# Value products of head pairs of 64: both heads in the column halves, in plain single precision

## What is computed

```python
# a: chunked attention over 9 chunks of 64 keys, with a relative bias (4 heads)
sc = einsum(qc, kb) * d ** -0.5 + bias
o = einsum('bhcqk,bckhd->bcqhd', softmax(sc), vb)
# b: each query attends the keys that an indexer picked (4 heads)
att = einsum('bqhd,bqkhd->bhqk', qb, ks) * scale
o = einsum('bhqk,bqkhd->bqhd', softmax(att), vs)
# d: neighbourhood of 8 rows by 16 columns plus 256 context keys (8 heads, odd layer)
p = softmax(concatenate([s_loc + bias, s_ctx]))
o = einsum(p_loc, vs) + einsum(p_ctx, vc)
```

## Time and profile before

| | |
|---|---|
| median of 3 runs | 4104.63 us (4094.35 to 4112.15) |
| profiled execution | 4107.38 us, span 4105.6 us |
| mean granted TensorE clock | 0.934 of 2.4 GHz |
| TensorE busy | 3635.7 us, 89% |
| weight loads | 3008.8 us, 73% |
| VectorE busy | 2167.0 us, 53% |
| ScalarE busy | 1415.1 us, 34% |
| POOL busy | 237.5 us, 6% |
| DMA | 230.08 MB, mean 56 GB/s |

### The profile page before, as it was taken

The page is one execution under the profiler, slowest core; times in us unless marked ns, Lnnn a source line. Parts: engine busy times, 40 slices in busy tenths (PEclk is TensorE's granted clock), DMA queues, the critical chain, the costliest instruction groups (busy, mean ns, idle before and its releaser), DMA issues. The chain is left out here.

```text
span 4105.6 us, 46423 instructions
## 1 busy us (share of the span) xinstructions
PE 3635.7 (89%) x19222; PEld 3008.8 (73%) x19222; DVE 2167.0 (53%) x3943; ACT 1415.1 (34%) x2519; POOL 237.5 (6%) x343
## 2 busy tenths in 40 slices
PE   7999998886989999999898888888698888988788
PEld 5888876765768888888676676776686777776667
DVE  4599944555734322323555655655535556525563
ACT  3211254444222211112345434444424445423441
POOL 1021110000100000000000000000000000000000
PEclk9699999898999999999899998988798999989999
DMA  3223330001521111111210011000221000110112
GB/s 111 96 93 127 120 118 23 28 21 60 181 83 48 51 36 52 52 46 40 90 34 23 23 33 32 27 28 22 80 74 65 31 30 30 37 31 8 32 34 95
DMA packets 69571, 230.08 MB, mean 56 GB/s; under 512 B 8744, under 2 KB 12840, under 8 KB 69360
## 3 DMA queue, kind: packets, MB, share of 16 engines
q1 hardware_dynamic: 43056, 132.68, 9.8%
q0 software_dynamic: 22848, 81.85, 5.8%
q10 hardware_dynamic: 3456, 12.58, 0.8%
HBM read 180.42 MB, written 36.17 MB: 53 GB/s over the span
## 5 line engine op out<-in xcount | busy, mean ns | idle before, releaser
L2388 PE MATMUL PS<-m,m 128*128 128x512 f32 (+3 forms) x3560 | 1413.2, 398 | 125.7 <-ACT m L2597 22.2
L2389 PE MATMUL PS<-m,m 128*128 128x512 f32 (+3 forms) x3560 | 1375.6, 388 | 0.0
L2390 PE MATMUL PS<-m,m 128*128 128x512 f32 (+3 forms) x3560 | 1373.4, 387 | 0.0
L2388 PEld LDWEIGHTS PS<-m,m 128*128 128x128 f32 (+2 forms) x3560 | 684.8, 193 | 304.0 <-ACT m L2597 31.3
L2390 PEld LDWEIGHTS PS<-m,m 128*128 128x128 f32 (+2 forms) x3560 | 686.0, 193 | 135.6 <-issue 1.6
L2389 PEld LDWEIGHTS PS<-m,m 128*128 128x128 f32 (+2 forms) x3560 | 688.8, 194 | 117.3 <-issue 2.3
L2735 DVE TENSOR_TENSOR m<-m,m 128x1024 fp32r<-128x1024 f32 (+5 forms) x204 | 210.2, 1031 | 400.2 <-ACT m L2573 399.5
L3021 DVE TENSOR_TENSOR m<-PS,m 128x512 fp32r<-128x512 f32 x352 | 240.9, 689 | 296.6 <-ACT m L2665 296.2
L2665 ACT CAST m<-PS 128x512 fp32r<-128x512 f32 x352 | 205.4, 589 | 495.9 <-PE PS L2495 494.4
L2486 PE MATMUL PS<-m,m 64*128 64x256 f32 (+5 forms) x1968 | 253.7, 369 | 70.6 <-ACT m L2654 54.1
L2486 PEld LDWEIGHTS PS<-m,m 64*128 64x128 f32 (+1 forms) x1968 | 214.8, 199 | 115.3 <-ACT m L2654 69.2
(11 more groups left out here) (196 smaller groups left out, 3897.0 us busy)
## 6 DMA issues: line engine op xcount, KB each, us to landing
m<-in_w SPq DMA_DIRECT2D x220, 512.0 KB, 3.5
g_scratch<-m ACTq DMA_DIRECT2D x24, 512.0 KB, 2.6
m<-g_scratch POOLq DMA_DIRECT2D x24, 512.0 KB, 4.7
m<-in_w SPq DMA_DIRECT2D x32, 256.0 KB, 2.6
x_scratch<-m POOLq DMA_DIRECT2D x2, 4096.0 KB, 13.5
m<-m POOLq DMA_DIRECT2D x60, 128.0 KB, 2.7
m<-in_xT POOLq DMA_DIRECT2D x24, 256.0 KB, 7.0
y_scratch<-m POOLq DMA_DIRECT2D x12, 512.0 KB, 2.9
```

Source lines behind the costliest of these rows:

```text
L2388: pe.e.engine.matmul(o, L[0], X[0], start=start, stop=False)
L2389: pe.e.engine.matmul(o, L[0], X[1], start=False, stop=False)
L2390: return pe.e.engine.matmul(o, L[1], X[0], start=False, stop=stop)
```

## The change

The unit is no longer cut into two parts. A group is one key tile for both heads: four transposes (head 0's two query blocks, head 1's two), one copy without rounding to a plain `pth`, by ScalarE for even groups and by VectorE for odd ones, and two plain matmuls: the 64 value columns of head i as weights, head i's 256 columns of `pth` as the moving operand, into rows 64i to 64i+63 of the output bank. The output is copied out once, 128 rows. `ptl`, `vl` and the subtractions go. All four buffers of a unit are given back with its last group. In the odd layer all six buffers are memory of their own, and the reload of the tables goes. Attentions with one head of 128 are as before.

```diff
-    def __init__(self, p, mem, s_banks, pt_banks, o_banks, fill_banks, E, second=()):
+    def __init__(self, p, mem, s_banks, pt_banks, o_banks, fill_banks, E, second=(), two=False):
...
-        self.pth = [mem([P, 512], R) for _ in range(2)]
-        self.ptl = [mem([P, 512], R) for _ in range(2)]
+        self.two = two
+        self.pth = [mem([P, 512], F if two else R) for _ in range(2)]
+        self.ptl = [None if two else mem([P, 512], R) for _ in range(2)]
...
     def queue(self, u):
-        fr = [f for f in u["fronts"] if "first" not in f]
-        kts = u["keys"]
-        groups = [kts[i:i + 2] for i in range(0, len(kts), 2)]
+        two = self.two
+        fr = u["fronts"][0::2] + u["fronts"][1::2] if two else [f for f in u["fronts"] if "first" not in f]
+        kts, size = u["keys"], 1 if two else 2
+        groups = [kts[i:i + size] for i in range(0, len(kts), size)]
...
-            blocks = [f["E"][:, e0:e0 + 128] for e0, _, _ in groups[g] for f in fr]
+            blocks = [f["E"][:, kt[0]:kt[0] + 128] for kt in groups[g] for f in fr]
             i = 128 * len(blocks)
+            on = ("act", "dve")[g % len(("act", "dve"))] if two else "act"
+            done = (self.S.lo, ("pt", un, g)) if on == "dve" or not two else (self.S.hi, ("pt", un, g))
...
-            self.p.bank_free[b] = [(self.S.lo, ("pt", un, g))]
+            self.p.bank_free[b] = [done]
             self.pt_free[r] = [(self.S.pv, (un, g))]
             if g == len(groups) - 1:
                 for f in fr:
                     self.e_free[f["e"]] = [(self.S.turn, (un, g))]
                     self.e_busy.discard(f["e"])
...
+            if two:
+                rows = [slice(64 * i, 64 * i + 64) for i in range(2)]
+                lead = [(O[rows[i], :], groups[g][0][1][:, rows[i]], h[i], g == 0, last) for i in range(2)]
+                rest = []
...
-            for part in u.get("parts", [u]):
-                self.queue(part)
+            self.queue(u)
...
-            vh, vl = mem([P, 8, 128], R), mem([P, 8, 128], R)
+            vt = mem([P, 8, 128])
...
-            at = Attention(p, mem, [[0, 1], [2, 3]], [4, 5], [6], [7], E_a)
+            at = Attention(p, mem, [[0, 1], [2, 3]], [4, 5], [6], [7], E_a, two=True)
...
-                    halves = [slice(64 * i, 64 * i + 64) for i in range(2)]
-                    units.append({"fronts": fronts, "parts": [
-                        {"fronts": fronts[i::2], "keys": [(128 * (y - lo), vh[:, y, :], vl[:, y, :]) for y in tiles],
-                         "evac": (yt[halves[i], 128 * b0:128 * b0 + 256], halves[i], None, [])} for i in range(2)]})
+                    units.append({"fronts": fronts, "keys": [(128 * (y - lo), vt[:, y, :]) for y in tiles],
+                                  "evac": (yt[:, 128 * b0:128 * b0 + 256], slice(0, P), None, [])})
...
-        at = Attention(p, mem, [[0, 1], [2, 3]], [4, 5], [6], [7], [mem([P, T]) for _ in range(4)] + [tabs[:, i, :] for i in range(2)])
+        at = Attention(p, mem, [[0, 1], [2, 3]], [4, 5], [6], [7], [mem([P, T]) for _ in range(6)], two=True)
...
-    t_tab = move(tabs[:, :, :], tab_d[1].rearrange("a p t -> p a t"))
...
         elif s.kind == "pv":
-            g, O = s["g"], s["O"]
-            pe.wait_ge(S.hi, ("pt", s["u"], g))
+            if s["rest"]:
+                pe.wait_ge(S.hi, ("pt", s["u"], s["g"]))
+            else:
+                pe.wait_ge(*s["there"])
             for ev in s["free"]:
                 pe.wait_ge(*ev)
-            for i, (vh, vl, h, l) in enumerate(s["terms"]):
-                e.matmul(O, vh, h, start=g == 0 and i == 0, stop=False)
-                e.matmul(O, vl, h, start=False, stop=False)
-            pe.wait_ge(S.lo, ("pt", s["u"], g))
-            for i, (vh, vl, h, l) in enumerate(s["terms"]):
-                m = e.matmul(O, vh, l, start=False, stop=s["last"] and i == len(s["terms"]) - 1)
-            m.then_inc(*pe.says(S.pv, (s["u"], g)))
+            for O, L, X, start, stop in s["lead"]:
+                m = e.matmul(O, L, X, start=start, stop=stop)
+            if s["rest"]:
+                pe.wait_ge(*s["there"])
+            for O, L, X, stop in s["rest"]:
+                m = e.matmul(O, L, X, start=False, stop=stop)
+            m.then_inc(*pe.says(S.pv, (s["u"], s["g"])))
...
-        elif s.kind == "turn":
+        elif s.kind == "turn" and s["on"] == "dve":
+            dve.wait_ge(S.turn, (s["u"], s["g"]))
+            for ev in s["free_pt"]:
+                dve.wait_ge(*ev)
+            e.tensor_copy(s["h"], s["src"]).then_inc(*dve.says(S.lo, ("pt", s["u"], s["g"])))
+        elif s.kind == "turn" and s["l"] is not None:
             dve.wait_ge(S.hi, ("pt", s["u"], s["g"]))
```

More of the change, by code:

```diff
@@ L442, in turn_over, with multiply @@
                     self.e_busy.discard(f["e"])
-            return r
-        def multiply(g, r):
+            return r, done
+        def multiply(g, r, there):
             last = g == len(groups) - 1
-            self.p.add("pv", u=un, g=g, free=(self.p.bank_free[ob] if g == 0 else []) + self.v_after, last=last, O=O,
-                       terms=[(vh, vl, self.pth[r][:, 256 * i:256 * i + 256], self.ptl[r][:, 256 * i:256 * i + 256])
-                              for i, (_, vh, vl) in enumerate(groups[g])])
+            h, l = ([None if x is None else x[:, 256 * i:256 * i + 256] for i in range(2)] for x in (self.pth[r], self.ptl[r]))
+            if two:
[3 more added lines that the diff above has]
+            else:
+                lead = [(O, v, h[i], g == 0 and i == 0 and v is kt[1], False) for i, kt in enumerate(groups[g]) for v in kt[1:]]
+                rest = [(O, kt[1], l[i], last and i == len(groups[g]) - 1) for i, kt in enumerate(groups[g])]
+            self.p.add("pv", u=un, g=g, free=(self.p.bank_free[ob] if g == 0 else []) + self.v_after, lead=lead, rest=rest,
+                       there=there)
             self.v_after.clear()
@@ L1531, in steps @@
                         yield from value_steps(at.fill_banks)
-                        yield from token_major_steps(zv, 8, [(vh, vl, 0, 0, 128)], ev["v"], at.fill_banks, at.v_after)
+                        yield from token_major_steps(zv, 8, [(vt, None, 0, 0, 128)], ev["v"], at.fill_banks, at.v_after)
                     for k_, j_ in nxt:
@@ L1553, in schedule @@
                     v_fill.drain()
-                    ready += to_token_major(zv, 8, [(vh, vl, 0, 0, 128)], ev["v"])
+                    ready += to_token_major(zv, 8, [(vt, None, 0, 0, 128)], ev["v"])
                     p.fence()
@@ L2121, in steps @@
             def steps():
-                yield from token_major_steps(zv, 10, [(vh, vl, 0, 0, 128)], ev["v"], at.fill_banks, at.v_after)
+                yield from token_major_steps(zv, 10, [(vt, None, 0, 0, 128)], ev["v"], at.fill_banks, at.v_after)
                 yield from next_steps(CHO, nxt, at.fill_banks)
@@ L2152, in schedule @@
                 kt = [(768, 8), (896, 9)] + [(128 * (y - tiles[0]), y) for y in tiles]
-                halves = [slice(64 * i, 64 * i + 64) for i in range(2)]
-                units.append({"fronts": fronts, "parts": [
-                    {"fronts": fronts[i::2], "keys": [(e0, vh[:, y, :], vl[:, y, :]) for e0, y in kt],
-                     "evac": (yt[halves[i], 128 * b0:128 * b0 + 256], halves[i], None, y_free)} for i in range(2)]})
+                units.append({"fronts": fronts, "keys": [(e0, vt[:, y, :]) for e0, y in kt],
+                              "evac": (yt[:, 128 * b0:128 * b0 + 256], slice(0, P), None, y_free)})
             units[1]["hook"] = hook
@@ L2192, in schedule @@
                        norm_bufs(1, 3, 2, half))
-            p.add("ready", on="dve", after=[t_tab])
-            p.add("ready", on="pool", after=[t_tab])
             post([(zr, P, CH2, None, "swap32", rph, rpl, er.events)], tmp)
@@ L2660, in scalar_program @@
             m.then_inc(*act.says(S.exp, n))
-        elif s.kind == "turn":
+        elif s.kind == "turn" and s["on"] == "act":
             act.wait_ge(S.turn, (s["u"], s["g"]))
@@ L2772, in vector_program @@
             e.tensor_tensor(s["z"], s["x"], s["y"], ALU.add).then_inc(*dve.says(S.rot, ("sum", n)))
-        elif s.kind == "tok":
+        elif s.kind == "tok" and s["parts"][0][1] is not None:
             for i, (vh, vl, o) in enumerate(s["parts"]):
```

16 lines of the change are left out of this document (8 added, 8 removed).

## The result

The changed kernel takes 4066.4 us (median of 6, 4057.1 to 4076.0), the kernel before beside it 4105.7 us (6 runs). The ratio is 0.9904, interval 0.9878 to 0.9929: 39 us faster, where 18 us slower had been forecast.

The account below looks back on a forecast made before the run. TensorE, busy 89%, was taken to bound the filled stretches, a chain through three engines b1 and d3. Terms 9 - 10 + 11 + 4 + 5 = +19 us on 4107.4 gave 4126, 4123 against the median; range 4070 to 4165.

Parts of the forecast that it names:

- The order of the groups, with its clock: All eight head-pair stretches: late-freed probability buffers force groups ahead of the maximum; +11 in b1 and d3, +4 filled, +5 clock.
- the five drops of the clock: In d3 and b1: five TensorE gaps of 3.7 to 4.7 us may halve the clock, 1 us each, +5.
- The products: TensorE-bound tiles, 156 of 188: two half-column matmuls plus shape change take 1.20 us a tile against 1.14, +9 us.
- the border: Every key tile: entering and leaving the half-array shape costs TensorE 0.31 to 0.36 us, 62 us over 188 tiles.
- the 6 us of the tails of d0 to d2: Near the end of each: a value product's 3.28 us wait for a queued VectorE subtraction shrinks, -2 us each, -6.
- the 4 of the first block: First block's stretches: shorter waits for the subtraction and for the shared output bank shrink, -4 us.
- Copies: Probability copies and value subtractions: VectorE and ScalarE relieved, almost none of it on the path in d0 to d2; -10 us.
- Rival A: All tiles: the array's shape change is free, 51 us less in the bound stretches, 4073 us; chance 0.12.
- Rival B: Second pair of 24 units: forced groups idle TensorE in filled stretches too, full half-clock cost, 4155 us; chance 0.37.
- forced groups: Second pair of units: without a free probability buffer, all remaining groups of the previous unit run ahead of VectorE's maximum.
- Rival C: Value products: the two halves do not run side by side, a tile's products take 0.87 us, +67, 4190 us; chance 0.04.
- 1408 and 752 records: Sign in the trace: transposes keep 1408 records, the new value products show 752 records of 128x64 weights.

Follow-up runs that it names:

- the order alone: Kernel before, products and copies untouched, with all remaining groups of the previous unit run at each unit's second score pair, ahead of its maximum: 4116.4 us, 1.0019.
- both parts put back: Changed kernel with VectorE's 188 subtractions and 20 operations on token-major values put back, products waiting for ScalarE alone: 4113.2 us, 1.0015.
- the token step: Changed kernel with VectorE's two-operand operation on the 20 token-major value blocks put back, holding the only fill bank until it ends: 4092.2 us, 0.9964.

## Why the prediction was wrong

The forecast went from 4107 by +19; the change did -39. In ratios to before the runs part the way as follows (0.1% is 4.1 us).

- **The order of the groups, with its clock** (11 + 4 + 5 = +20 forecast): +8 by the run with the order alone, interval 4 to 12. d3 and b1 came out as worked out, 15 us where 11 and the five drops of the clock made 16; d0 to d2 cost 6. Missed was that the same groups give 10 us in a0 and a1; in a1 they cover a gap.
- **The products** (9 us more on TensorE): the price per tile was right, 1.21 and 1.17 us against 1.20, and so was the border of 0.31 to 0.36, by the trace and by two runs that take it away or halve it. With the 6 us of the tails of d0 to d2 (a product waiting 3.28 us for a subtraction, gone now) and the 4 of the first block, the forecast for this part was -1, and the run gave -2 with an uncertainty of some 7. That they agree is partly luck: by the traces the -2 is 9 us more in b1 and d3 and more than that less elsewhere. The Trainium skill, TensorEngine Tiling (Array Packing), Key Properties, has the drain at a change of mode, and the trace agrees; how much it is, only the rows said.
- **VectorE's relief**: the step that failed, in the term *Copies*. "None of it is on the path in d0 to d2 but for one wait" priced 188 subtractions and 20 more at -10 us, and these 10 are in the -1 above, since the kernels with the copy work put back are rid of that wait too. Put back one by one the two cost another 21 to 23 us and 23 to 25. So 46 us stand where the forecast had nothing, or 38 by the spans of the two profiled executions. The traces place 35 of them: 15 in the gaps, 10 in b1 and d3, 6 in d0 to d2 and 4 in a0, a1 and b0. The 10 in b1 and d3 are a shorter chain, which the forecast did count in its +11 there (against it, the products with the grouping cost 9 in the same place, and in b1 and d3 together the forecast's 16 met 14). What it missed outright are the gaps and d0 to d2.

The three parts are 8, -2 and -46, by runs that each differ from the next in one of them; that they add up to the measured -39 follows from that and is no further evidence.

The clock is part of it too. The forecast counted it in b1 and d3 alone. From the start of d0 to the start of d1 the granted clock is 0.94 before and 0.98 after, 0.94 with both parts put back and 0.95 with the token step; of the 8.4 us between before and after there, 5.6 are time in which TensorE sat idle.

The error was in how waits were looked for. I took the share of TensorE in d0 (84.3 of 89 us) as proof that its instructions are the time there, and looked for VectorE's waits inside the eight stretches. The gaps between them, 20 to 31 us each, are part of the same stage, and a wait of 4.26 us stood in each of two of them, with the subtraction's own line as the releaser. And VectorE at half load is still a queue: the mean says nothing of the 1.9 us between the end of ScalarE's copy and a subtraction that sits behind other stages' work, while a single bank is held.

Two views would have shown it: TensorE's waits for VectorE over the whole of the first block and the last layer, grouped by the line waited for, and then for each subtraction that the change removes, what it holds. The Trainium skill, Perfetto Trace Analysis, Optimization Strategy, says that the same gap repeating on the engine that should be saturated can mean too few buffers for the next tile. Here that rule points at the right place: the gap stood behind both d0 and d1 (4.26 and 4.25 us), and the resource was one PSUM bank. A second fill bank was not tried.

Rival A's 4073 is close to the time measured, and its mechanism is wrong: the border of the array is not free, a tile takes 1.21 us and not 0.87. Rival B was right that forced groups cost in filled stretches, but by 2 us in each of d0 to d2, and in a0 and a1 they gave. Rival C fell with the first row of L2509: four records of 64 weight columns take 0.58 us to the next line.

Of the forecast's signs these held: 1408 and 752 records, the step near 1.2 us, waits of 3 to 5 us for the exponentials in d3 (3.98 and 4.35, each with a shorter one of 1.3 to 1.5 ahead of it), ScalarE -64, d0 to d2 within 3 us of before, d3 +10. Those that fell: VectorE -69 instead of -83, and a kernel that is faster all the same. A new wait that was not forecast is the one for the normalisation at the end of a stretch (4.0 us in d3, 4.6 in a1, 5.1 in b1): with both heads in one unit, the first transposes wait for the last head.

## What to carry to other kernels

When a change takes work off an engine that is not the bound, list what each removed instruction holds (a bank, a buffer, a place in a queue) and who waits for that, also in the seams between stages; half-busy engines have queues where stages meet. A single bank that two engines must pass in turn kept the bound engine waiting up to 4.3 us a time here, against 1.7 with one, and freeing it one engine earlier was worth about as much (17 to 25 us for 20 instructions) as the other 188 subtractions (21 to 23). Where a matmul shape differs from its neighbours', group several of the kind: some 0.3 us a tile for going in and out here, and 23 us in all by doing so once for two tiles.

## What was not expected of the hardware

- VectorE's one-operand copy of 128x512 from PSUM takes 691 ns and its two-operand subtraction 689, while the one-operand operation in SBUF is at 487: dropping an operand saves nothing when the other comes from PSUM. The Trainium skill, VectorE: DVE Perf Modes, Why PSUM operands drop a tier, says that an fp32 operation with an operand in PSUM stays at the base rate; the rows agree.
- A gap of 2.14 us behind score matmuls was followed by 17 us at 1.2 GHz, two of 0.94 and 0.85 us (eight buffers everywhere) by 13 us of it, and one of 4.6 us by some 3. In these traces the length of the gap alone does not say how long the clock stays down.
